# One lookup per pick from a joined expert table, and the second half summed through diagonals on TensorE

## The chip, the core and the metric

The kernel runs on one core of a Trainium2 chip. The metric is the device time of one execution in microseconds, as the median of several runs. The profiles come from single profiled executions of the same program.

## The reference

Two layers of a diffusion backbone for 128 prompt tokens and 256 sample tokens. Each layer is a mixer (attention of two kinds and a short convolution, between projections) and then a feed-forward part in which every token looks up experts by product keys. The change concerns this second part, which the reference computes for chunks of 128 tokens, eight heads and sixteen picks a head:

```python
def one_chunk(xc):
    q = (xc @ wq).reshape(P_CHUNK, P_HEADS, 2, P_HALF)
    sc = jnp.einsum('thcd,hcnd->thcn', q, sub_keys).astype(jnp.float32)
    s1, i1 = lax.top_k(sc[:, :, 0], P_TOPK)
    s2, i2 = lax.top_k(sc[:, :, 1], P_TOPK)
    ...
    top_s, pos = lax.top_k(cand, P_TOPK)
    eidx = jnp.take_along_axis(cand_idx, pos, axis=-1)
    gate = jax.nn.softmax(top_s, axis=-1).astype(xc.dtype)
    u = jnp.take(u_tab, eidx, axis=0)
    act = jax.nn.gelu(jnp.einsum('thkd,td->thk', u, xc))
    vv = jnp.take(v_tab, eidx, axis=0)
    return jnp.einsum('thk,thkd->td', gate * act, vv)
```

All is float32. A token has 8 x 16 = 128 picks, each a row of 1024 values (4 KB) of `u_tab` and one of `v_tab`. Over two layers and three token tiles of 128 tokens that is 2 x 3 x 128 = 768 picks of 128 tokens each, 805 MB out of tables of 16384 rows a layer.

## The kernel before

Tokens lie on the 128 partitions, in three tiles (`T = 3`): tile 0 is the prompt, tiles 1 and 2 the samples. A layer's dense work (norms, projections, attention, output projection, queries and their scores against the keys) is written per group of tiles as a generator `dense_stages(l, tiles)` on each engine, cut into steps; the four stages are P0, S0, P1 and S1 (layer and group). P0's first part runs alone. The rest runs beside the lookups: `Beside` gives each step a weight and calls the next steps whenever their due share of the items is reached. Every engine walks the same list, so that order is fixed by hand and is the same on all of them.

A tile's picks are cut into two units of 64 (`UNIT`), twelve in all. `segments()` lists which unit's first half ("u") and which unit's second half ("v") run together, and beside which dense pieces. `route(n)` on VectorE finds the sixteen picks of a head with searches (L1602 to L1636). The first half: GpSimd issues an indirect DMA that brings row `picks[token]` of `peer_u` to each token's partition, 128 rows of 4 KB (L815), and VectorE multiplies it with the token's activations and sums (`dot`, L1663, with a read of the accumulator). After 64 dots `coefficients(unit)` makes GELU times gate (L1670 to L1679), with ScalarE's tanh (L1278) in the middle. The second half goes another way: TensorE transposes the coefficients (`turn`, L1078) and the picks' numbers (`turn_rows`, L1066), so that the 64 picks of two tokens lie on the 128 partitions; each lookup of `peer_v` (L815 too) brings all picks of a pair of tokens; ScalarE spreads the coefficients over mostly zero columns (`spread`, L1315); and TensorE sums four such lookups at a time with 128x32 matmuls on the four column groups of the array (`add_rows`, L1095) into `ps_acc`. At the end of a tile `feed` (L1687 to L1691) takes the sum, scaled by the modulation gate (a broadcast matmul, L838), into `x`.

Both kinds of lookup share a ring of 14 slots of 4 KB a partition (`RING`); its memory also serves as three extra homes for dense weights before the lookups begin. `lookups()` writes out the order in which GpSimd issues them, and `free_slot` makes it wait for the slot's last reader: VectorE for a "u", TensorE for a "v". The weights come in chunks of 2 MB on SyncE's queue. In float32 a matmul shows as two MATMUL instructions in the profile.

Of the kernel before, what the change touches and what calls it, by code (L numbers as in the profile page):

```python
# [46 lines left out]
HOME_ROWS = KC * NB // DM  # L47
UNIT_HEADS = P_HEADS // 2
UNIT = UNIT_HEADS * TOPK
UNITS_ALL = DEPTH * T * 2  # L50
RING = 14
LEAD = 14
LAG = 12
QUADS = 4
QROWS = P // QUADS
PER = P // UNIT
PARTS = 4
PART = UNIT // PARTS
SPREAD = PART * QROWS + QROWS
GATE_AT = UNIT - 12  # L60
EARLY_ROWS = (1, 5, 7, 11)
ROWS_AT = UNIT - 8
ROWS_HEAD = 2
ROWS_PQ = 9
AHEAD = 2
ROWS = 12
# [29 lines left out]


def after_out(tiles):

    return steps(tiles).index("out") + OUT_CHUNKS * len(tiles)  # L100


SPARSE = 2 * QUADS
EARLY, LATE = (0, UNIT // 2), (UNIT // 2, UNIT)
# [57 lines left out]

class Beside:


    def __init__(self, pieces, programs, items):
        self.steps = [(programs[piece.stage], weight) for piece in pieces for weight in piece.weights]
        self.share = sum(weight for _, weight in self.steps) / items
        self.due, self.done, self.at = 0.0, 0, 0

    def step(self):
        program, weight = self.steps[self.at]
        next(program)
        self.done += weight
        self.at += 1

    def item(self):
        self.due += self.share
        while self.at < len(self.steps) and self.done < self.due - 1e-6:
            self.step()  # L180

    def end(self):
        while self.at < len(self.steps):
            self.step()


class Segment:

    def __init__(self, u, v, beside=None, last=False, rows=(0, UNIT)):
        self.u, self.v, self.beside, self.last = u, v, beside, last
        self.first_row, self.end_row = rows
        self.items = UNIT if u is not None else self.end_row - self.first_row
        self.begins = v is not None and self.first_row == 0
        self.ends = v is not None and self.end_row == UNIT
        self.lag = LAG if u is not None and self.begins else 0
        self.next_u = None

    def rows_added(self, i):  # L200

        if self.v is None:
            return None
        if self.u is not None and self.first_row:
            return self.first_row + i // SPARSE * QUADS if i % SPARSE == SPARSE - 1 else None
        return self.first_row + i - self.lag - QUADS + 1 if i % QUADS == QUADS - 1 and i >= self.lag else None


P0, S0, P1, S1 = (0, P_TILES), (0, S_TILES), (1, P_TILES), (1, S_TILES)


def pieces(name):

    if name is None:
        return (), 1
    if name == "start":
        return (Piece(P0, 0, split_at(P_TILES)),), 1
    if name == "s0_first":
        return (Piece(P0, split_at(P_TILES), None, 2.5), Piece(S0, 0, S0_HALF)), UNIT
    if name == "s0_last":  # L220
        return (Piece(S0, S0_HALF, after_out(S_TILES)),), UNIT
    if name == "s0_end":
        return (Piece(S0, after_out(S_TILES), split_at(S_TILES)),), UNIT // 2
    if name == "s0_rest":
        return (Piece(S0, split_at(S_TILES)),), REST_ITEMS
    if name == "p1":
        return (Piece(P1),), 3 * UNIT + 20
    if name == "s1_first":
        return (Piece(S1, 0, S1_HALF),), UNIT
    if name == "s1_last":  # L230
        return (Piece(S1, S1_HALF, after_out(S_TILES)),), UNIT
    if name == "s1_end":
        return (Piece(S1, after_out(S_TILES), split_at(S_TILES)),), UNIT // 2
    return (Piece(S1, split_at(S_TILES)),), REST_ITEMS


def segments():

    order = (Segment(0, None, "s0_first", True), Segment(1, 0, "s0_last", True),
             Segment(None, 1, "s0_end", True, EARLY), Segment(2, 1, "s0_rest", True, LATE),  # L240
            Segment(3, 2, "p1"), Segment(4, 3, "p1"), Segment(5, 4, "p1"), Segment(None, 5, "p1", True),
            Segment(6, None, "s1_first", True), Segment(7, 6, "s1_last", True),
             Segment(None, 7, "s1_end", True, EARLY), Segment(8, 7, "s1_rest", True, LATE),
            Segment(9, 8), Segment(10, 9), Segment(11, 10), Segment(None, 11))
    for g, after in zip(order, order[1:]):
        g.next_u = after.u
    return order


REST_ITEMS = 40  # L250
S0_HALF = 23
S1_HALF = 20
# [63 lines left out]


HOME, LATEST = homes()
ADA_ORDER = {which: n for n, which in enumerate(c for c in CHUNKS if c[0] == "ada")}

# [50 lines left out]
def pair_of(i):  # L371

    return UNIT // QUADS * (i % QUADS) + i // QUADS
# [1445 lines left out]
```

## Time and profile before

| | |
|---|---|
| time, median of 3 runs (lowest to highest) | 2635.54 us (2628.28 to 2641.29) |
| span of the profiled execution | 2775.9 us |
| bytes moved | 963.23 MB, mean 347 GB/s |
| TensorE, VectorE, GpSimd, ScalarE busy | 1502.5, 1580.1, 1580.2, 284.8 us |
| mean granted clock of TensorE | 0.719 |

The profiled execution is known by its span, from the first to the last instruction; no time around it is shown, so the span is taken as its own time. It is 5.3% above the median of the other runs, and sums made from its rows are brought to that median by the ratio. In the profile a row's first number is busy time (overlaps counted once), then the mean length of one instruction; the idle time behind it is that of the engine just before such instructions. "DMA share" is the mean busy share of sixteen DMA engines. The granted clock is a share of 2.4 GHz.

### The profile page before, as it was taken

To read this page: it belongs to the slowest core of one execution; us is meant where nothing else is said; L and a number is where in the kernel's file an instruction comes from. 1 tells how busy PE (TensorE), PEld (TensorE's weight loads), DVE (VectorE), ACT (ScalarE), POOL (GpSimd) and SP (SyncE) were. 2 spreads that over 40 slices of the span, in tenths; PEclk is the share of its full clock that TensorE was granted. 3 is DMA by queue.
4 is the path that set the end of the run, shared out by engine and by line. 5 is a ranking of instruction groups with operands and counts; after the bars stand their busy time and mean duration, and the time that the engine had idled before them with its cause. 6 is when DMAs were issued, how large, how long until landed. Compare 5 with 4: busy or idle time off the path is not lost.

```text
span 2775.9 us, 21719 instructions
## 1 busy us (share of the span) xinstructions
PE 1502.5 (54%) x6476; PEld 657.2 (24%) x6476; DVE 1580.1 (57%) x3734; ACT 284.8 (10%) x736; POOL 1580.2 (57%) x1601
## 2 busy tenths in 40 slices
PE   6776766867626443445456776686642332232345
PEld 2254323424402111112222234333420000000011
DVE  1348958633767656647446578652668656547410
ACT  1211012211001001000000102211000000000000
POOL 0016526665555566664566785665556666666664
PEclk9888866788857765567777895788865656565567
DMA  9959987899899999998999997999979999999998
GB/s 362 387 204 392 370 310 270 306 371 364 309 381 353 395 357 359 357 353 320 349 369 404 338 391 275 327 333 354 363 292 376 363 359 348 356 364 358 362 372 305
DMA packets 299013, 963.23 MB, mean 347 GB/s; under 512 B 28280, under 2 KB 30712, under 8 KB 298128
## 3 DMA queue, kind: packets, MB, share of 16 engines
q0 software_dynamic: 221184, 805.40, 77.0%
q1 hardware_dynamic: 77712, 156.44, 15.5%
q8 instruction: 53, 0.87, 0.1%
q14 instruction: 64, 0.52, 0.1%
HBM read 959.12 MB, written 2.62 MB: 346 GB/s over the span
## 4 chain that ended last, share of the span: by engine, by line
PE 26%; DMA 19%; DVE 16%; issue 16%; POOL 11%; another core or an unknown queue 10%; ACT 1%; SPq 0%; POOLq 0%; DVEq 0%; ACTq 0%
POOL ring L815 11%; DMA ring<-peer_v,v_rows 9%; PE ps_acc L1095 8%; DVE ring L1663 8%; PE ps_mm L899 5%; DMA ring<-peer_u,u_rows 4%; PE ps_mm L1050 3%; DMA ring<-ada_w 2%; DMA weights<-w_in 2%; PE ps_mm L1020 2%; PE ps_mm L954 2%; DMA weights<-ada_w 1%; PE ps_mb L982 1%; PE ps_acc L858 1%
## 5 line engine op out<-in xcount | busy, mean ns | idle before, releaser
L815 POOL DMA_INDIRECT ring<-peer_v,v_rows x768 | 751.5, 978 | 588.2 <-issue 215.8
L815 POOL DMA_INDIRECT ring<-peer_u,u_rows x768 | 806.1, 1050 | 383.2 <-issue 207.3
L1095 PE MATMUL ps_acc<-ring,coef_cols 128*32 128x512 f32 x3072 | 589.0, 907 | 800.5 <-DMA ring<-peer_v,v_rows 785.8
L1663 DVE CUSTOM_DVE_ANT_0 ring<-ring,ps_tr 128x1024 f32<-128x1024 f32 x512 | 616.6, 1220 | 419.3 <-DMA ring<-peer_u,u_rows 347.8
L1095 PEld LDWEIGHTS ps_acc<-ring,coef_cols 128*32 128x32 f32 x3072 | 117.3, 143 | 1181.4 <-issue 1178.6
L1663 DVE CUSTOM_DVE_ANT_0 ring<-ring,h 128x1024 f32<-128x1024 f32 x256 | 304.9, 1221 | 24.0 <-DMA ring<-peer_u,u_rows 14.7
L1050 PE MATMUL ps_mm<-hT,weights 128*128 128x128 f32 (+1 forms) x1024 | 202.0, 353 | 23.9 <-issue 23.2
L899 PE MATMUL ps_mm<-weights,hT 128*128 128x512 f32 x432 | 199.0, 622 | 17.8 <-DMA weights<-w_in 13.4
L1050 PEld LDWEIGHTS ps_mm<-hT,weights 128*128 128x128 f32 x1024 | 170.8, 211 | 74.6 <-issue 61.4
L776 POOL TENSOR_SCALAR u_rows<-picks 128x16 uint32<-128x16 f32 x48 | 15.9, 330 | 204.2 <-DVE picks L1636 203.2
L899 PEld LDWEIGHTS ps_mm<-weights,hT 128*128 128x128 f32 x432 | 85.5, 200 | 130.8 <-issue 108.9
L1687 DVE TENSOR_TENSOR h<-h,ps_acc 128x1024 f32<-128x1024 f32 x6 | 7.3, 1219 | 190.5 <-PE ps_acc L1095 147.9
L1040 PE MATMUL ps_mb<-proj 128*128 128x128 f32 x160 | 30.7, 314 | 106.5 <-ACT proj L1263 103.3
L954 PE MATMUL ps_mm<-h,scores 32*128 32x384 f32 (+1 forms) x144 | 73.5, 750 | 17.2 <-ACT scores L1208 9.1
L1502 DVE TENSOR_REDUCE negmax<-ps_mm 128x1 f32<-128x384 f32 (+1 forms) x108 | 47.8, 464 | 58.8 <-PE ps_mm L954 35.8
L1020 PE MATMUL ps_mm<-weights,hT 128*128 128x512 f32 x160 | 74.3, 618 | 0.0
L1602 DVE MAX8 half_top<-scores 128x8 f32<-128x128 f32 x96 | 23.3, 284 | 86.6 <-ACT scores L1257 45.6
L1315 ACT ACTIVATE coef_cols<-turned 64x16 f32<-64x16 f32 x96 | 21.9, 228 | 443.8 <-PE ps_acc L1095 386.8
L858 PE MATMUL ps_acc<-weights,condT 128*32 128x512 f32 x224 | 40.4, 862 | 49.8 <-DMA weights<-ada_w 49.8
L1208 ACT ACTIVATE scores<-ps_mm,negmax 128x384 f32<-128x384 f32 (+1 forms) x108 | 54.4, 508 | 107.3 <-DVE negmax L1502 93.2
L1263 ACT ACTIVATE proj<-ps_mm 128x128 f32<-128x128 f32 (+1 forms) x64 | 21.1, 331 | 429.6 <-remote 250.1
L1663 DVE DVE_READ_ACCUMULATOR2_ANT dots<- 128x1 f32 x768 | 63.3, 82 | 0.0
(218 smaller groups left out, 1525.9 us busy)
## 6 DMA issues: line engine op xcount, KB each, us to landing
weights<-w_in SPq DMA_DIRECT2D x17, 2048.0 KB
weights<-peer_wq SPq DMA_DIRECT2D x16, 2048.0 KB
weights<-ada_w SPq DMA_DIRECT2D x14, 2048.0 KB
ring<-ada_w SPq DMA_DIRECT2D x10, 2048.0 KB, 18.0
ring<-peer_u,u_rows POOLq DMA_INDIRECT x768
weights<-w_out SPq DMA_DIRECT2D x6, 2048.0 KB
ring<-peer_v,v_rows POOLq DMA_INDIRECT x768
ring<-w_in SPq DMA_DIRECT2D x3, 2048.0 KB, 20.7
```

The lines of the kernel that those rows point to most:

```text
L815: pool.indirect_dma_start(ring[:, place % RING, :], None, src, bass.IndirectOffsetOnAxis(ap=rows, axis=0)).then_inc(row_full[place % RING] ...
L858: last = pe.matmul(ps_acc[QROWS * j:QROWS * (j + 1), n % 2 * NB:(n % 2 + 1) * NB], condT[:, k, at:at + QROWS], w[:, k, :], start=(i == 0), ...
L899: last = pe.matmul(mm(i), hT[:, k, j * P:(j + 1) * P], w[:, k, :], start=(k == 0), stop=(k == KC - 1))
L954: pe.matmul(scores_at(l, tiles, g, nk * P), q, k, start=True, stop=True, tile_position=(lo, 0)).then_inc(score_mm, 1)
L982: last = pe.matmul(ps_mb[:, col:col + HD], w_.probsT[:, head % 2, s * P:(s + 1) * P], v, start=(s == 0), stop=(s == nk - 1))
L1020: pe.matmul(mm(i), hT[:, k, j * P:(j + 1) * P], w[:, k, :], start=(k == 0), stop=(k == KC - 1))
L1040: last = pe.matmul(key_scores_at(l, tiles, i, nt * P)[:, j * P:(j + 1) * P], pqT[:, i % 4, j * P:(j + 1) * P], keysT[:, i, :], start=True, ...
L1050: last = pe.matmul(mm(i, nt * P), w[:, k, (i % 4) * P:(i % 4 + 1) * P], hT[:, k, 0:nt * P], start=(k == 0), stop=(k == KC - 1))
L1095: last = pe.matmul(ps_acc[QROWS * k:QROWS * (k + 1), b * NB:(b + 1) * NB], coef_cols[:, i // PART % 2, at:at + QROWS], ring[:, slot("v", n ...
L1208: act.activation(w_.probs[:, probs_slot(head, second), 0:nk * P], scores_at(l, tiles, g, nk * P), ACT.Exp, bias=negmax[:, u:u + 1], accum_ ...
L1502: dve.tensor_reduce(negmax[:, u:u + 1], scores_at(l, tiles, j * UNITS + u, nk * P), AXX, ALU.max, negate=True).then_inc(negmax_ready, 1)
L1663: dve.tensor_tensor_reduce(row, row, h, 1.0, 0.0, ALU.mult, ALU.add, dots[:, n // UNIT % 2, n % UNIT:n % UNIT + 1]).then_inc(u_used, 1)
```

## The change

The tables `peer_u` and `peer_v` become one table a layer, `peer_uv0` and `peer_uv1`, whose row is 8 KB: the u row and behind it the v row. One lookup a pick brings both to the token's partition, 1 MB a lookup. The ring has 9 slots of 8 KB a partition (`SLOTS`). Rows are no longer turned to other partitions: TensorE adds `diag(coefficient of pick n) @ v rows of pick n` into `ps_acc`, with two 128x128 matmuls of 512 columns a pick, whose diagonal ScalarE makes from the identity and the coefficient as a scale (`diagonals`). Coefficients are made for two picks at a time (`GROUP = 2`): `polynomial(g)` behind the second dot, tanh on ScalarE, `coefficients(g)` behind the dense steps of that item. TensorE adds a pair one pair later (`LATE_GROUPS = 1`). Gates are handled per head, with the sum taken by the exponential. `segments()` and `lookups()` go; one loop over 768 picks remains, with the dense pieces at ranges of picks (`sides()`). Modulation sums of later stages go to `ps_mb`, because `ps_acc` is in use from the first pick on. The area for the lookups' descriptors is given as 4096 bytes.

```diff
-RING = 14
-LEAD = 14
-LAG = 12
+SLOTS = 9
+HOME_SLOTS = KC * NB // (2 * DM)
+TILE = P_HEADS * TOPK
+PICKS = DEPTH * T * TILE
...
+GROUP = 2
+LATE_GROUPS = 1
+FEED_AT = 2
+DIAGS = 6
 AHEAD = 2
...
+def sides():
+
+    return ((0, 104, (Piece(P0, split_at(P_TILES), None, 2.5), Piece(S0, 0, split_at(S_TILES)))),
+            (TILE, TILE + 40, (Piece(S0, split_at(S_TILES)),)),
+            (TILE + 40, 3 * TILE - 32, (Piece(P1),)),
+            (3 * TILE + 4, 3 * TILE + 104, (Piece(S1, 0, split_at(S_TILES)),)),
+            (4 * TILE, 4 * TILE + 40, (Piece(S1, split_at(S_TILES)),)))
...
@@ gpsimd
-            for place, (table, n) in enumerate(LOOKUPS):
-                if table == "u":
-                    if n % TOPK == 0:
-                        take_head(n // TOPK)
...
+            for n in range(PICKS):
+                if n % TOPK == 0:
+                    pool.wait_ge(picks_ready, n // TOPK + 1)
                     pool.sem_inc(gather_may, 1)
...
+                if n >= SLOTS:
+                    pool.wait_ge(v_used, n - SLOTS + 1)
+                    pool.sem_inc(gather_may, 1)
+                picks = rows[:, n // TOPK % HEADS_KEPT, n % TOPK:n % TOPK + 1]
+                pool.indirect_dma_start(ring[:, n % SLOTS, :], None, peer_uv1 if n >= PICKS // 2 else peer_uv0,
+                                        bass.IndirectOffsetOnAxis(ap=picks, axis=0)).then_inc(row_full[n % SLOTS], 16)
@@ tensor
-                for b in range(2):
-                    for k in range(QUADS):
-                        at = (k * PART // QUADS + r % (PART // QUADS) + 1) * QROWS - PER - PER * r
-                        last = pe.matmul(ps_acc[QROWS * k:QROWS * (k + 1), b * NB:(b + 1) * NB],
-                                         coef_cols[:, i // PART % 2, at:at + QROWS], ring[:, slot("v", n + k), b * NB:(b + 1) * NB],
-                                         start=(r == 0), stop=(r == UNIT // QUADS - 1), tile_position=(0, QROWS * k))
-                last.then_inc(v_used, QUADS)
+                pe.wait_ge(diag_ready, n + 1)
                 for b in range(2):
+                    last = pe.matmul(ps_acc[:, b * NB:(b + 1) * NB], diags[:, n % DIAGS, :],
+                                     ring[:, n % SLOTS, DM + b * NB:DM + (b + 1) * NB], start=(i == 0), stop=(i == TILE - 1))
+                last.then_inc(v_used, 1)
...
+            for i in range(PICKS):
+                side.item(i)
+                if i % GROUP == GROUP - 1 and i // GROUP >= LATE_GROUPS:
+                    add_group(i // GROUP - LATE_GROUPS)
+                if i >= TILE and i % TILE == FEED_AT - 1:
+                    gate_sum_rows(i // TILE - 1)
@@ scalar
+            def diagonals(g):
+                act.wait_ge(coef_ready, g + 1)
+                for n in range(g * GROUP, (g + 1) * GROUP):
+                    if n >= DIAGS:
+                        act.wait_ge(v_used, n - DIAGS + 1)
+                    act.activation(diags[:, n % DIAGS, :], ident, ACT.Copy, scale=of_head(coef, n)).then_inc(diag_ready, 1)
@@ vector
+            def polynomial(g):
+
+                n = g * GROUP
+                a, some = of_head(dots, n, GROUP), of_head(poly, n, GROUP)
+                dve.wait_ge(u_used, n + GROUP)
+                step.after(dve.scalar_tensor_tensor(out=some, in0=a, scalar=GELU_A, in1=a, op0=ALU.mult, op1=ALU.mult))
+                dve.scalar_tensor_tensor(out=some, in0=some, scalar=1.0, in1=a, op0=ALU.add, op1=ALU.mult).then_inc(poly_ready, 1)
...
+                step.after(dve.scalar_tensor_tensor(out=of_head(gated, n, GROUP), in0=a, scalar=gate_inv[:, head % 2:head % 2 + 1],
+                                                    in1=gates_of(head)[:, k:k + GROUP], op0=ALU.mult, op1=ALU.mult))
+
+            def coefficients(g):
+
+                n = g * GROUP
+                dve.wait_ge(tanh_ready, g + 1)
+                dve.scalar_tensor_tensor(out=of_head(coef, n, GROUP), in0=of_head(poly, n, GROUP), scalar=1.0,
+                                         in1=of_head(gated, n, GROUP), op0=ALU.add, op1=ALU.mult).then_inc(coef_ready, 1)
...
+                dot(i)
+                if i % GROUP == GROUP - 1:
+                    polynomial(i // GROUP)
+                side.item(i)
+                if i % GROUP == GROUP - 1:
+                    coefficients(i // GROUP)
+                if i >= TILE and i % TILE == FEED_AT:
+                    feed(i // TILE - 1)
@@ kernel()
-    arrays["peer_u"] = a["peer_u"].reshape(DEPTH * N_EXPERTS, DM)
-    arrays["peer_v"] = a["peer_v"].reshape(DEPTH * N_EXPERTS, DM)
+    for l in range(DEPTH):
+        arrays[f"peer_uv{l}"] = np.concatenate([a["peer_u"][l], a["peer_v"][l]], axis=1)
```

## Rows read from the trace of the kernel before

**Rows 1.** Busy time of the engines, from the page.

```profile
PE 1502.5 (54%) x6476; PEld 657.2 (24%) x6476; DVE 1580.1 (57%) x3734; ACT 284.8 (10%) x736; POOL 1580.2 (57%) x1601
```

**Rows 2.** DMA queues: packets, MB, share of sixteen engines' span.

```profile
q0 software_dynamic: 221184, 805.40, 77.0%
q1 hardware_dynamic: 77712, 156.44, 15.5%
```

**Rows 3.** By stretch: us, PE, PEld, DVE, ACT, POOL busy; clock, DMA share, GB/s.

```profile
0.00:200.00 200.00, 144.74 (x679) 70.07 (x680) 59.62 (x163) 34.18 (x93) 3.40 (x7) 0.86 0.86 314
200.00:672.00 472.00, 345.91 (x1388) 174.50 (x1387) 312.47 (x729) 81.49 (x193) 266.47 (x242) 0.78 0.92 339
...
1549.00:1950.00 401.00, 296.66 (x1108) 145.80 (x1108) 251.45 (x494) 77.91 (x179) 264.99 (x232) 0.81 0.91 335
...
2130.00:2776.00 646.00, 219.65 (x1038) 44.57 (x1038) 310.35 (x715) 13.03 (x46) 415.31 (x446) 0.62 0.95 355
```

**Rows 4.** A window of 20 us with lookups alone.

```profile
2120.00:2140.00 20.00, 0.80 (x3) 0.20 (x2) 18.41 (x41) 1.63 (x7) 14.48 (x17) 0.58 1.02 410
```

**Rows 5.** DMA queues of four stretches: 0:200, 200:672, 1549:1950, 2130:2776.

```profile
q1 hardware_dynamic: 32222, 62.71, 86.2%
...
q0 software_dynamic: 32968, 120.07, 68.6%
q1 hardware_dynamic: 19426, 39.52, 22.9%
...
q0 software_dynamic: 31976, 116.41, 78.6%
q1 hardware_dynamic: 8665, 17.62, 11.9%
...
q0 software_dynamic: 62716, 228.34, 94.2%
```

**Rows 6.** Windows of L1095 alone: PE and PEld busy.

```profile
200.00:672.00 472.00, 64.11 (x384) 12.99 (x384) 0.78 0.92 339
1549.00:1950.00 401.00, 60.64 (x368) 12.33 (x368) 0.81 0.91 335
```

**Rows 7.** Pieces of the chain: start us, us, what.

```profile
1830.13 7.06 PE ps_mm L1020 x16
...
2116.88 3.49 PE ps_acc L838 x4
```

**Rows 8.** Waits of PE, 200:672: us in total, times, longest.

```profile
PE ps_acc L858 <- DMA weights<-ada_w: 29.4, 6, 12.7
...
PE ps_tr L877 <- DVE merged L1410: 8.0, 2, 6.2
```

**Rows 9.** Waits of PE, 1549:1950.

```profile
PE ps_mm L899 <- DMA weights<-w_in: 9.3, 2, 4.7
PE ps_tr L877 <- DVE h L1410: 8.3, 2, 6.9
```

**Rows 10.** Groups of instructions: busy us, mean ns, idle before.

```profile
L1663 DVE CUSTOM_DVE_ANT_0 ring<-ring,ps_tr 128x1024 f32<-128x1024 f32 x512 | 616.6, 1220 | 419.3 <-DMA ring<-peer_u,u_rows 347.8 <-issue 33.1 <-remote 18.8
L1663 DVE DVE_READ_ACCUMULATOR2_ANT dots<- 128x1 f32 x768 | 63.3, 82 | 0.0
L1509 DVE RECIPROCAL rinv<-rowsum 128x2 f32<-128x2 f32 x36 | 5.8, 160 | 2.0 <-ACT scores L1208 1.6 <-issue 0.3
L1297 ACT ACTIVATE turned<-ps_acc 128x128 f32<-128x128 f32 x12 | 3.3, 278 | 2.3 <-PE ps_acc L1078 1.6 <-issue 0.5
```

**Rows 11.** Timeline of VectorE: end of one head's routing and of the next.

```profile
1448.99 0.19 DVE L1636 SCALAR_TENSOR_TENSOR picks<-pair_key 128x32 f32<-128x32 f32 x1
...
1458.17 0.19 DVE L1636 SCALAR_TENSOR_TENSOR picks<-pair_key 128x32 f32<-128x32 f32 x1
```

**Rows 12.** Timeline: one unit's coefficients, first and last operation.

```profile
2278.92 0.23 DVE L1670 TENSOR_TENSOR poly<-dots 128x64 f32<-128x64 f32 x1
...
2280.04 0.29 DVE L1679 SCALAR_TENSOR_TENSOR coef<-poly,dots 128x128 f32<-128x128 f32 x1 [0.25 <-issue]
```

More of the change, by code:

```diff
@@ L160, in __init__ @@
         self.weights = [weight or weights[kind] for kind in kinds[first:last]]
-class Beside:
[L166 to L184, printed above, removed]
@@ L187 @@
[L187 to L206, printed above, removed]
@@ L209 @@
[L209 to L234, printed above, removed]
@@ L237, in segments @@
[L237 to L247, printed above, removed]
@@ new lines, with __init__, item @@
+class Beside:
+    def __init__(self, programs):
+        self.programs, self.at = programs, [0] * len(sides())
+        self.done = [0.0] * len(sides())
+    def item(self, i):
+        for s, (first, end, pieces) in enumerate(sides()):
+            if not first <= i < end:
+                continue
+            order = [(piece.stage, weight) for piece in pieces for weight in piece.weights]
+            due = sum(weight for _, weight in order) * (i + 1 - first) / (end - first)
+            while self.at[s] < len(order) and (self.done[s] < due - 1e-6 or i == end - 1):
+                stage, weight = order[self.at[s]]
+                next(self.programs[stage])
+                self.done[s] += weight
+                self.at[s] += 1
@@ L255, in ada, with start @@
+def start(programs):
+    for _ in range(split_at(P_TILES)):
+        next(programs[P0])
 def ada(l, first, last):
@@ L842, in modulate @@
             def modulate(which):
-                assert not made["turned"]
                 made[which[0]] += 1
@@ L971, in weigh_values @@
                             pe.wait_ge(conv_read, nth(l, tiles, 1, j))
-                        if head == A_HEADS and j == nt - 1 and early_row(l, tiles) is not None:
-                            pe.wait_ge(rows_ready, early_row(l, tiles) + 1)
                         for s in range(nk):
@@ L996, in dense_stages @@
                             weigh_values(head - 2)
-                        if early_row(l, tiles) is not None and j == nt - 1 and head == ROWS_HEAD:
-                            turn_rows(early_row(l, tiles))
                         yield "head"
@@ L1224, in dense_stages @@
                             exps(head + 1)
-                        if early_row(l, tiles) is not None and j == nt - 1 and head == ROWS_HEAD:
-                            copy_rows(early_row(l, tiles))
                         yield "head"
@@ L1265, in dense_stages @@
                         copy_scores(i - 1)
-                    if (l, tiles) == P1 and i == ROWS_PQ:
-                        copy_rows(2 * T - 1)
                     if i == 15:
@@ new lines, in _ @@
+            start(programs)
+            side = Beside(programs)
+            for n in range(AHEAD):
+                for _ in route(n):
+                    pass
+                if n == 0:
+                    gate_top(0)
+            routing = iter(())
+            for i in range(PICKS):
+                head, k = i // TOPK, i % TOPK
+                if k == TOPK // 2:
+                    for _ in routing:
+                        pass
+                    routing = route(head + AHEAD) if head + AHEAD < ALL_HEADS else iter(())
+                next(routing, None)
+                if k == 2 and head + 1 < ALL_HEADS:
+                    gate_top(head + 1)
+                dot(i)
+                if i % GROUP == GROUP - 1:
+                    polynomial(i // GROUP)
+                side.item(i)
+                if i % GROUP == GROUP - 1:
+                    coefficients(i // GROUP)
+                if i >= TILE and i % TILE == FEED_AT:
+                    feed(i // TILE - 1)
```

435 lines of the change are left out of this document (98 added, 337 removed).

## The prediction

> **What bounds the kernel now.** The order of reading was the page's busy line, its DMA queues, and then windows by stretch; groups, waits and pieces of the chain came after them, for durations. TensorE, VectorE and GpSimd are each busy for 54 to 57% of the span [rows 1], but the lookups' queue fills 77.0% of the sixteen DMA engines' time and the weights' queue 15.5% [rows 2]: together 92.5% of 2775.9 us. The windows [rows 3] tell the stretches apart. Lookups start at about 200 us. In the stretch that is nearly lookups alone, 2130 to 2776, the DMA share is 0.95 at 355 GB/s with PE at 34% and DVE at 48%: transfers set the pace. In the two stretches that hold the sample tiles' dense work (200 to 672 and 1549 to 1950) the share drops to 0.92 and 0.91 while PE is busy for 73 and 74% of the time: there the dense work already costs transfers something. I call a "pick" one expert of 128 tokens with both its rows, 1.0486 MB; there are 768, before as two lookups and after as one.
>
> **Transfers.** Bytes don't change; packets do. Two queues give two equations: 221184 packets and 805.40 MB took 77.0% of 16 x 2775.9 us, and 77712 packets and 156.44 MB took 15.5% [rows 2]. They solve to 6.9 ns a packet and 40.6 us a MB of one engine's time. After, there are half as many lookup packets, so 110592 x 6.9 ns / 16 = 48 us of transfer time go. A pick falls from 2137/768 = 2.78 us to 2.72 us at a full DMA. Bounds: nothing gained (2.78), and the fastest window that shows only lookups, 410 GB/s at share 1.02 [rows 4], which is 2.56 us a pick before that saving and 2.50 after it. I take 2.72, because it stands on all packets. How full is the DMA? Now 0.95 in the lookup stretch. The ring goes from 14 half-size slots (7 MB) to 9 full ones (9 MB), and GpSimd, busy for 415 of 646 us there [rows 3], issues half as many lookups; I take 0.98, so 2.72/0.98 = 2.775 us a pick. The same stretch runs now at 646 us for 228.34 MB [rows 3, 5], 2.97 us a pick. GpSimd's own saving, half of its busy time, is worth nothing by itself: the transfers cover it.
>
> **TensorE.** Removed: the 128x32 matmuls (64.1 and 60.6 us busy in the two dense stretches [rows 6]) and the transposes of coefficients and rows. Added: each pick is two full 128x128 matmuls of 512 columns, and the chain shows how such a float32 matmul is two instructions: 16 took 7.06 us, 4 took 3.49 us [rows 7]. So a pick costs 4 instructions: 1.77 us at the 2.4 GHz level, 3.49 us where the engine had been mostly idle and the clock was at its lower level (1.2 GHz). 768 picks are 1359 us at the fast level, in place of 589. In the lookup stretches 1.77 is under 2.775 and hides; if the clock drops, PE falls behind, becomes busy, and the dense stretches show what a busy PE is granted (0.78 and 0.81 as means [rows 3]). In the dense stretches it doesn't hide. There PE has its own work in front of each pair of picks:
> - first sample stretch: 345.9 - 64.1 = 281.8 us of other PE work, which the new schedule spreads over picks 0 to 104; plus 104 x 1.77 = 184; plus waits that stay, 29.4 for modulation weights and 8.0 on VectorE [rows 8]: 503 us. Transfers alone would want 104 x 2.72 + 39.52 MB x 2.75 us = 392 us (2.75 us a MB is 430 us for 156.44 MB [rows 2]), so PE is the bound.
> - second: 296.7 - 60.6 = 236.0 us of other work, 100 picks x 1.77 = 177, waits 9.3 + 8.3 [rows 9]: 431 us, against 320 for transfers.
> Before, these stretches took 472 and 401 us and carried 120.07 and 116.41 MB [rows 3, 5], that is 114.5 and 111 picks. After, they carry fewer picks in more time. That is the loss which I set against the gain elsewhere.
>
> **VectorE and ScalarE.** Per pair of picks VectorE does two dots, 2 x (1.220 + 0.082) [rows 10]; one eighth of a head's routing, 9.18 us from one head's last operation to the next [rows 11]; and a chain of four small operations with a tanh of ScalarE in the middle, which now comes 384 times and not 12. Now it takes 1.41 us on 64 columns, from 2278.92 to 2280.33 [rows 12]. Two columns cost about what the reciprocal on two columns does, 160 ns [rows 10]; the bounds are 4 x 0.16 = 0.64 and 1.41; I take 1.0 us. With some 0.25 us of gaps a pair is 5.0 us, so 2.5 us a pick: under 2.775, but with only 10% to spare. If an operation or the wait for tanh costs more, what is late is the coefficient, then the diagonal, then the slot, which is not free before TensorE has read it. Behind the waiting coefficient stand the next dots and routing. ScalarE adds 768 diagonals at some 278 ns [rows 10] and 384 tanh: about 310 us on an engine that is 10% busy, at no cost to the end. The gate's maximum and exponential per head, the per-head reciprocal and one 1.2 us addition less per tile are within 20 us and hidden. The modulation sums that go to another PSUM tile wait for nothing new. The smaller descriptor area only matters if nine lookups in flight do not fit, for which nothing speaks.
>
> **The sum**, in the profiled execution's time: 200 up to the first lookup, as before; 503; 431; the other 768 - 204 = 564 picks x 2.775 = 1565; the weights outside the three named stretches, 156.44 - 62.71 - 39.52 - 17.62 = 36.6 MB [rows 2, 5] x 2.75 = 101; and 20 us for the end (the last pair's chain, its matmuls, gate and store). That is 2820 us against 2776, 1.6% more. The median of the runs, 2635.5, is 0.949 of the profiled span, so about **2677 us**.
>
> A rule that speaks against any gain stands in the Trainium skill, HBM Reference, "Specifications (TRN2)": some 358 GB/s effective per core. By it a pick could never take less than 2.93 us, whatever its packets; the 355 GB/s of the lookup stretch looks like it [rows 3], the 410 GB/s window disagrees [rows 4]. The case is rival 1, worked out there from rows alone.
>
> **Rivals.**
> 1. No gain per pick: lookups keep their present 2.97 us, because what limits them is not packets or issue. For it: PE, DVE and POOL all have room in that stretch and it still runs at 355 GB/s. Against: the 20 us window at 410 GB/s. Then 564 x 0.19 = 107 more: 2927, so 2779 us.
> 2. The faster side: picks outside the dense stretches run at the burst pace, 2.50/0.98 = 2.55 us. Place: those 564 picks; price -0.225 x 564 = -127 us; 2693, so 2557 us. It decides from 2.70 us a pick: there the sum equals 2776. For it: that window [rows 4], and the deeper ring. Against: VectorE's 2.5 us leaves nothing over. The Trainium skill (DMA: Bandwidth & Descriptors, "Where 436 GB/s comes from") gives a ceiling of 435 GB/s, by which a pick would take 2.41 us; no row reaches it.
> 3. A full-rate clock in the dense stretches. PE's other work there was measured at 0.78 and 0.81. Fully busy, it could shrink to at best 220 and 191 us, 107 us off: 2713, so 2576 us. For it: 0 to 200 us had 0.86 at 72% busy [rows 3]. Against: part of that work is small instructions and latencies that don't scale.
> 4. VectorE as the bound: pairs at 6.0 us, 3.0 a pick, 127 us more: 2947, so 2798 us. This takes 0.5 us a pick more than my count.
> 5. A slow clock throughout: the lookup stretch had 0.62 [rows 3]. If TensorE got no more than the 1.2 GHz level there, a pick would take 3.49 us: 564 x 0.715 = 403 more, 3223, so 3060 us. Against: busier stretches had 0.78 and more, and here PE would be busy all the time. The Trainium skill (TensorE: Matmul & The Clock Gate, Part 1) says that the low rate is the default and activity releases it; the trace agrees, with 0.62 where PE is busy 34% and 0.86 at 72% [rows 3].
>
> **How the numbers follow.** This kernel's runs spread over 0.5%, so less can't be told from no change: 2622 to 2649 us is "same". Chances: my forecast (2650 to 2750) 0.38; rival 2 or 3, alone or in part, 0.34; halves of them that end within 0.5%, 0.13; rival 1 0.07, rival 4 0.06, rival 5 0.02. So faster 0.34, same 0.13, slower 0.53. The range reaches down past rivals 2 and 3 (2557, 2576), leaving out that both hold fully, and up past 1 and 4: 2540 to 2800. The forecast's own range is 2650 to 2750.
>
> **What would show it.** Lookup packets at 110592 and the queue's share times span near 2090 us; in the last stretch a pick per 2.7 to 2.8 us with DMA share 0.97 or more. The stretch from the first lookup to pick 104 near 500 us, PE busy over 90% of it, GpSimd idle for TensorE; DMA share there under 0.85. PE busy in total over 2000 us. VectorE at 2.5 us a pick in lookup stretches. The prediction is wrong if PE's other work shrinks with a faster clock, if packets cost more than 6.9 ns each, or if VectorE's small chain costs over 1.5 us a pair.

## The result, and the profile after

The changed kernel takes 2686.8 us (median of 4 runs, 2686.34 to 2690.32) beside 2634.3 us for the kernel before on the same chip: a ratio of 1.0204, 95% interval 1.0184 to 1.0223. It is 2% slower on that chip; the experiments show that this side doesn't hold on every chip. On two later occasions it took 2690.4 and 2686.9 us, with ratios of 1.0217 and 1.0209. The forecast was 2677 us.

From the page of the changed kernel: its span, the busy line, and the lookups' and weights' queues (packets, MB, share of sixteen engines). They answer to [rows 1, 2].

```profile
span 2684.8 us, 23465 instructions
...
PE 2230.6 (83%) x6452; PEld 1073.4 (40%) x6452; DVE 1793.1 (67%) x5249; ACT 600.2 (22%) x1836; POOL 789.9 (29%) x773
...
q0 software_dynamic: 110592, 805.36, 74.7%
q1 hardware_dynamic: 77712, 156.44, 15.9%
```

Half the lookup packets and the same bytes, as the change says; TensorE's busy time grows by 728 us and GpSimd's halves, against [rows 1].

The same page, groups of the new work (busy us, mean ns, idle before and what ended it):

```profile
L904 PE MATMUL ps_acc<-ring,diags 128*128 128x512 f32 x3072 | 1456.2, 624 | 218.2 <-ACT diags L1084 215.2
L656 POOL DMA_INDIRECT ring<-peer_uv,rows x768 | 787.9, 1026 | 1864.6 <-PE ps_acc L904 1515.5
...
L1077 ACT ACTIVATE poly<-poly 128x2 f32<-128x2 f32 x384 | 77.6, 202 | 1163.3 <-DVE poly L1414 1163.1
L1084 ACT ACTIVATE diags<-consts,coef 128x128 f32<-128x128 f32 x768 | 265.5, 393 | 115.9 <-DVE coef L1425 113.7
L1425 DVE SCALAR_TENSOR_TENSOR coef<-poly,gated 128x2 f32<-128x2 f32 x384 | 61.9, 161 | 221.5 <-ACT poly L1077 220.0
```

GpSimd has become a waiter: 1515.5 us of its idle time end when TensorE has read a slot. That alone doesn't say that TensorE is the bound, since with a full ring this wait is there too when transfers set the pace. The windows decide. Windows of the changed kernel (us; PE, PEld, DVE, ACT, POOL busy; clock, DMA share, GB/s): the start, the stretch from the first lookup to pick 104, the second sample stretch (picks 388 to 488), and the lookups alone at the end. They answer to [rows 3].

```profile
0.00:200.00 200.00, 139.89 (x640) 65.52 (x641) 56.82 (x152) 34.56 (x92) 2.30 (x6) 0.89 0.86 312
200.00:695.00 495.00, 427.91 (x1407) 219.71 (x1407) 301.58 (x840) 123.18 (x346) 126.90 (x108) 0.92 0.82 305
...
1539.00:1955.00 416.00, 375.08 (x1123) 190.10 (x1122) 281.84 (x788) 115.74 (x320) 113.96 (x98) 0.95 0.77 289
...
2128.00:2670.00 542.00, 417.44 (x871) 166.30 (x869) 418.26 (x1259) 101.27 (x347) 202.56 (x211) 0.96 1.00 412
```

And the lookups' queue in the last three of these stretches (packets, MB, share), which answers to [rows 5]:

```profile
q0 software_dynamic: 15280, 111.29, 59.4%
...
q0 software_dynamic: 14021, 102.11, 65.0%
...
q0 software_dynamic: 30627, 222.99, 99.5%
```

The kernel before was profiled again on a chip on which it takes as long as in the timed runs above (2632 us). Its span there is 2627.2 us. The same stretches and queue rows of that execution:

```profile
200.00:665.00 465.00, 341.26 (x1398) 171.72 (x1397) 313.65 (x735) 83.25 (x199) 268.94 (x243) 0.79 0.93 345
1485.00:1885.00 400.00, 307.17 (x1151) 152.83 (x1152) 257.74 (x521) 79.09 (x183) 261.33 (x233) 0.80 0.92 339
...
2044.00:2600.00 556.00, 204.15 (x978) 40.95 (x974) 294.70 (x677) 13.02 (x46) 399.54 (x432) 0.61 1.01 392
```

```profile
q0 software_dynamic: 33080, 120.50, 69.3%
...
q0 software_dynamic: 32159, 117.10, 79.2%
...
q0 software_dynamic: 59748, 217.57, 100.4%
```

**Where the time went.** The two sample stretches went from 465 and 400 us with 120.50 and 117.10 MB of lookups to 495 and 416 us with 111.29 and 102.11 MB. At 1.0486 MB a pick that is 46 us more for 23 picks fewer, and those picks cost 2.6 us each later on: 106 us lost. Elsewhere the kernel before took 2627 - 200 - 865 = 1562 us for 541 picks, the changed one 2685 - 200 - 911 = 1574 us for 564. With some 98 us for weights in both, a pick falls from 2.70 to 2.62 us, which gives 48 us back. The difference is the 58 us between the two spans. The ends of the stretches are read by hand (in two executions of one kernel, further below, the first came to 454 and 448 us), so the split is good to some 6 us. At the end, with lookups alone, a pick falls from 556/207.5 = 2.68 to 542/212.7 = 2.55 us.

### The profile page after: what moved, and what is told of

Its sections match the earlier page's. It is cut to its first block, busy times and chain, and to the rows that moved or that the text cites. A ratio compares the mean times of both kernels' runs of the same rounds, so it can differ in the third digit from the quotient of the medians.

```text
span 2684.8 us, 23465 instructions
## 1 busy us (share of the span) xinstructions
PE 2230.6 (83%) x6452; PEld 1073.4 (40%) x6452; DVE 1793.1 (67%) x5249; ACT 600.2 (22%) x1836; POOL 789.9 (29%) x773
## 3 DMA queue, kind: packets, MB, share of 16 engines
q0 software_dynamic: 110592, 805.36, 74.7%
HBM read 959.12 MB, written 2.62 MB: 358 GB/s over the span
## 4 chain that ended last, share of the span: by engine, by line
PE 47%; DMA 22%; DVE 21%; issue 5%; ACT 3%; POOL 1%; SPq 0%; DVEq 0%; POOLq 0%; ACTq 0%
PE ps_acc L904 24%; DMA ring<-peer_uv,rows 17%; DVE ring L1406 8%; PE ps_mm L739 7%; PE ps_mm L886 5%; PE ps_mm L858 3%; DMA ring<-ada_w 2%; PE ps_mm L796 2%; POOL ring L656 1%; DMA weights<-w_in 1%; DMA weights<-peer_wq 1%; DMA weights<-ada_w 1%; PE ps_mb L679 1%; DVE poly L1413 1%; ACT poly L1077 1%
## 5 line engine op out<-in xcount | busy, mean ns | idle before, releaser
L904 PE MATMUL ps_acc<-ring,diags 128*128 128x512 f32 x3072 | 1456.2, 624 | 218.2 <-ACT diags L1084 215.2
L656 POOL DMA_INDIRECT ring<-peer_uv,rows x768 | 787.9, 1026 | 1864.6 <-PE ps_acc L904 1515.5
L904 PEld LDWEIGHTS ps_acc<-ring,diags 128*128 128x128 f32 x3072 | 591.5, 199 | 997.7 <-issue 645.9
L1077 ACT ACTIVATE poly<-poly 128x2 f32<-128x2 f32 x384 | 77.6, 202 | 1163.3 <-DVE poly L1414 1163.1
L1084 ACT ACTIVATE diags<-consts,coef 128x128 f32<-128x128 f32 x768 | 265.5, 393 | 115.9 <-DVE coef L1425 113.7
L1425 DVE SCALAR_TENSOR_TENSOR coef<-poly,gated 128x2 f32<-128x2 f32 x384 | 61.9, 161 | 221.5 <-ACT poly L1077 220.0
L886 PE MATMUL ps_mm<-hT,weights 128*128 128x128 f32 (+1 forms) x1024 | 188.4, 341 | 17.6 <-DMA weights<-peer_wq 9.3
L1418 DVE SCALAR_TENSOR_TENSOR gated<-dots,gate_inv,pair_top 128x2 f32<-128x2 f32 x384 | 83.0, 216 | 1.7
L1414 DVE SCALAR_TENSOR_TENSOR poly<-poly,dots 128x2 f32<-128x2 f32 x384 | 62.2, 162 | 13.4
L1413 DVE SCALAR_TENSOR_TENSOR poly<-dots 128x2 f32<-128x2 f32 x384 | 61.7, 161 | 13.3
L796 PE MATMUL ps_mm<-h,scores 32*128 32x384 f32 (+1 forms) x144 | 49.3, 543 | 11.1 <-ACT scores L1009 7.5
## 6 DMA issues: line engine op xcount, KB each, us to landing
ring<-ada_w SPq DMA_DIRECT2D x10, 2048.0 KB, 16.6
```

The costliest lines, as they stand in the source:

```text
L656: pool.indirect_dma_start(ring[:, n % SLOTS, :], None, peer_uv1 if n >= PICKS // 2 else peer_uv0, bass.IndirectOffsetOnAxis(ap=picks, axis ...
L796: pe.matmul(scores_at(l, tiles, g, nk * P), q, k, start=True, stop=True, tile_position=(lo, 0)).then_inc(score_mm, 1)
L886: last = pe.matmul(mm(i, nt * P), w[:, k, (i % 4) * P:(i % 4 + 1) * P], hT[:, k, 0:nt * P], start=(k == 0), stop=(k == KC - 1))
L904: last = pe.matmul(ps_acc[:, b * NB:(b + 1) * NB], diags[:, n % DIAGS, :], ring[:, n % SLOTS, DM + b * NB:DM + (b + 1) * NB], start=(i == ...
L1077: act.activation(some, some, ACT.Tanh, scale=GELU_B).then_inc(tanh_ready, 1)
L1084: act.activation(diags[:, n % DIAGS, :], ident, ACT.Copy, scale=of_head(coef, n)).then_inc(diag_ready, 1)
```

## The experiments

**Is the kernel before the same everywhere?** Two runs of it, unaltered.

> The kernel before, unchanged, profiled once more. Theory: its first profiled execution (span 2775.9 us) was slower than its runs, because the one of the changed kernel has a span of 2684.8 us at a time of 2686.6 us. Then this one has a span of about its time, near 2635 us, and the 140 us are missing above all in lookup stretches, which then run above 355 GB/s. Rival: the profiler itself costs this kernel 5% (it has twice the lookups), then the span is near 2776 us again.

Measured: 2772.7 us (2756.58 to 2792.44) on one chip, span 2772.1.

> The kernel before, unchanged, for a profile that stands on the same chip as the others of this job. Its span should equal its time within 2 us, as in the last job (2772.1 at 2772.7). If it runs near 2634 us here, theory 1 wants its 4 KB packets shorter than the 172.8 ns mean of the slow chip's profiles, and its dense stretches hardly changed; rival 2 wants them longer or shorter everywhere.

Measured on another chip: 2631.9 us (2619.57 to 2642.61), span 2627.2. So the kernel before takes 2773 us on one chip and 2632 on another, and in both cases the profiled execution is as long as the timed ones. The first of the two expectations failed in both its theories: not only the profiled execution was long there, every timed run was. By their lengths, the span of 2775.9 us that the prediction was built on belongs to the first kind of chip and the median of 2635.5 to the second; which chips these were isn't known. Windows with lookups alone, on the first chip (columns as above), with their queue row:

```profile
2130.00:2700.00 570.00, 188.88 (x866) 37.68 (x870) 301.76 (x696) 12.57 (x44) 375.79 (x405) 0.59 0.96 361
...
q0 software_dynamic: 56514, 205.78, 96.2%
```

That is 570/196.2 = 2.90 us a pick, against 2.68 on the other chip. Only about half of this difference is longer packets: the queue's share times the time is 2.79 us a pick here and 2.69 there. The rest is time in which the DMA engines moved nothing (share 0.96 against 1.01).

**Does the joined lookup give the pace?** The changed kernel, but with the tables apart and two lookups of 4 KB rows a pick into the same slot:

```diff
-                pool.indirect_dma_start(ring[:, n % SLOTS, :], None, peer_uv1 if n >= PICKS // 2 else peer_uv0, ...)
+                for half in range(2):
+                    pool.indirect_dma_start(ring[:, n % SLOTS, half * DM:(half + 1) * DM], None, tables[half], ...)
...
-            return (n // SLOTS + 1) * 16
+            return (n // SLOTS + 1) * 32
```

> The changed kernel, but each pick takes two lookups of 4 KB rows from two tables into the two halves of its slot. Theory 1 (packets): a pick gets dearer by the 6.9 ns of 128 more packets, 0.06 us, which is 34 us over the 564 picks outside the dense stretches: about 2720 us, with lookup stretches at some 407 GB/s in place of 417. Rival 2 (depth of the ring alone): nothing changes, 2687 us within 10. Rival 3 (GpSimd): a lookup costs it 1.24 us from issue to issue, 2.48 us a pick, nearly the pace of 2.56 us, and with its waits it becomes the bound: 2.7 us a pick or more, over 2760 us.

Measured: 2848.0 us, beside 2772.8 for the kernel before on the same chip (the first kind), ratio 1.0294 (1.0234 to 1.0355). Windows of this kernel: the two sample stretches and the end.

```profile
200.00:699.00 499.00, 433.89 (x1395) 218.94 (x1395) 301.29 (x835) 122.68 (x345) 232.90 (x214) 0.90 0.84 302
1603.00:2020.00 417.00, 376.03 (x1125) 190.53 (x1124) 282.60 (x790) 116.46 (x320) 222.88 (x198) 0.95 0.81 291
2217.00:2830.00 613.00, 435.74 (x867) 175.44 (x865) 415.88 (x1258) 101.40 (x347) 399.93 (x422) 0.90 0.96 363
```

The sample stretches are nearly as long as in the changed kernel (499 and 417 against 495 and 416 us on the other kind of chip): there the form of the lookup hardly matters. The end falls back to 363 GB/s, the kernel before's pace on this chip (361), though the ring is 9 MB. So without the joined row the rest of the change costs 2.9% here, and the joined row gives the pace back. Its price is far above theory 1's 34 us, if the changed kernel takes some 2690 us on this chip too, and the time lies where rival 3 put it, over 2760 us. This run doubles two things at once, the packets and GpSimd's issues, and doesn't separate them. GpSimd was busy for 399.93 of 613 us at the end, and only 36 us of its idle time there were waits for a slot. On the faster chip the kernel before issued as many lookups a pick at 2.68 us a pick, so GpSimd's work alone doesn't explain the 2.89 us of this run; how the gain is shared between fewer packets and fewer issues stays open.

**What does TensorE's sum cost beside the dense work?** The second matmul of a pick (columns 512 to 1023 of the sum) is left out, for picks 0 to 103 and 384 to 487 in one kernel, and for all other picks in a second.

```diff
-                for b in range(2):
+                beside = 104 if tau in (0, 3) else 0
+                for b in range(1 if i < beside else 2):
```

> The changed kernel without the second of the two matmuls of a pick for picks 0 to 103 and 384 to 487, so columns 512 to 1023 of these picks are left out of the sum. Theory (TensorE is the bound of the two dense stretches): each of these 204 picks saves 0.88 us, 92 and 92 us at most; the first stretch falls from 495 to about 405 us, the second from 416 to about 330, and the time to about 2515 us. Rival (the waits between engines in the dense steps set these stretches, or the transfers do): under 40 us in all, 2650 us or more.

> The changed kernel without the second matmul of a pick everywhere but in the two dense stretches (picks 0 to 103 and 384 to 487) and at each tile's first and last pick; half of the columns of those picks are left out of the sum. Theory: TensorE is hidden behind transfers there, the time stays within 15 us of 2687 us. Rival (TensorE, 70 to 80% busy there, also bounds those stretches, with its wait for the late pair): the time falls by more than 60 us.

Measured: 2621.4 us for the first, 65 us less than the changed kernel, and 2670.3 us for the second, 17 us less though it leaves out nearly three times as many matmuls. Both ran on the first kind of chip and the changed kernel on the second; on a chip of the second kind the first of them took 2616.3 us (below), 71 us less than the changed kernel there. TensorE is the bound in the sample stretches and nearly hidden elsewhere. But the gain is far from the 2515 us expected: halving 373 us of sum in those stretches took 152 us off the sum's busy time and freed only 71. Windows of the first of the two kernels, and under them TensorE's work on `ps_acc` alone in the same windows:

```profile
200.00:654.00 454.00, 356.90 (x1188) 184.60 (x1187) 299.36 (x826) 122.53 (x345) 116.55 (x107) 0.87 0.86 329
1504.00:1890.00 386.00, 313.25 (x927) 160.71 (x926) 281.31 (x788) 115.67 (x320) 108.98 (x99) 0.88 0.82 315
```

```profile
200.00:654.00 454.00, 111.50 (x205) 0.87 0.86 329
1504.00:1890.00 386.00, 110.30 (x201) 0.88 0.82 315
```

The same two rows of the changed kernel:

```profile
200.00:695.00 495.00, 190.75 (x400) 0.92 0.82 305
1539.00:1955.00 416.00, 182.57 (x393) 0.95 0.77 289
```

In the first stretch TensorE's sum fell by 79 us and the stretch by 41. Its other work rose from 427.91 - 190.75 = 237 to 245 us at a lower granted clock (0.92 to 0.87), and its idle time from 67 to 97 us: more of the waits for weights and for other engines is uncovered, the one for modulation weights for example 22.1 us in place of 16.6.

**A cheaper form of the sum.** ScalarE scales the v row itself (128x1024, in place of the 128x128 diagonal) into a float32r tile, and TensorE adds it with the identity: one instruction for 512 columns in place of two. A slot is free as soon as ScalarE has read it, and no longer when TensorE has. Memory then holds 8 slots and not 9.

```diff
-SLOTS = 9
+SLOTS = 8
+SCALED = 2
...
-                    last = pe.matmul(ps_acc[:, b * NB:(b + 1) * NB], diags[:, n % DIAGS, :], ring[:, n % SLOTS, DM + ...], ...)
+                    last = pe.matmul(ps_acc[:, b * NB:(b + 1) * NB], ident_r[:], scaled[:, n % SCALED, b * NB:(b + 1) * NB], ...)
...
-                    act.activation(diags[:, n % DIAGS, :], ident, ACT.Copy, scale=of_head(coef, n)).then_inc(diag_ready, 1)
+                    act.activation(scaled[:, n % SCALED, :], ring[:, n % SLOTS, DM:], ACT.Copy, scale=of_head(coef, n)).then_inc(row_scaled, 1)
```

> The changed kernel with another way to the sum: ScalarE scales the v rows of a pick by its coefficient (128x1024, rounded to float32r) and TensorE adds them with the identity as two float32r matmuls, one instruction each. 8 slots in place of 9, two scaled buffers in place of six diagonals, and a slot is free as soon as ScalarE has read it. Theory (TensorE's 1.77 us a pick is what the dense stretches lack): TensorE falls to some 0.5 us a pick, 1300 us less in all; the first dense stretch goes from 495 to its other PE work and waits, about 380 to 420 us, the second from 416 to about 320 to 340, the rest stays, so about 2530 us. Rival (e2 took 92 us off each stretch and gave back only 48 and 30, so waits between engines and a slower clock take over): about 2600 us. Second rival: ScalarE's 1.0 us a pick in its fixed order delays the attention steps, over 2650 us.

Measured: 2618.7 us beside 2633.2 for the kernel before, ratio 0.9934 (0.9911 to 0.9958). It beats both, the kernel before by a little (0.7%). The time is near the first rival's 2600 us and not the theory's 2530; the sum took 743.6 us of TensorE in all, in place of 1456.2, which is 0.97 us a pick and 713 us less, where 0.5 us and 1300 us had been expected. Beside it the changed kernel ran again:

> The changed kernel, unchanged, beside the kernel before on one chip. The kernel before has now been seen at 2634 us and, in another job, at 2773 us. Theory 1 (chips differ in what lookups of 4 KB rows cost, and 8 KB rows don't feel it): the changed kernel takes 2687 us within 10 again, whatever the kernel before takes here, so the ratio is 1.02 where that is near 2634 and 0.97 where it is near 2773. Rival 2 (the slower chip is slower for both): 2687 x 1.05 = 2825 us where the kernel before takes 2773.

Measured: 2690.4 us, ratio 1.0217 (1.0178 to 1.0256). So this form is worth 72 us, the cheaper sum, the earlier release of the slot and the slot less taken together; no run separates them. Windows of the kernel with scaled rows, whole and for `ps_acc` on TensorE alone:

```profile
200.00:661.00 461.00, 350.57 (x1214) 206.76 (x1213) 301.22 (x837) 200.08 (x346) 114.81 (x110) 0.79 0.86 326
1498.00:1889.00 391.00, 313.05 (x931) 185.83 (x929) 281.57 (x787) 191.47 (x321) 107.10 (x99) 0.77 0.80 302
2061.00:2608.00 547.00, 244.75 (x432) 108.02 (x432) 418.25 (x1262) 262.62 (x349) 203.26 (x211) 0.50 0.99 411
```

```profile
200.00:661.00 461.00, 81.49 (x205) 0.79 0.86 326
```

TensorE's sum fell by 109 us in the first stretch, the stretch by 34. TensorE's other work rose from 237 to 269 us (clock 0.92 to 0.79) and its idle time from 67 to 110. At the end it ran at 1.2 GHz throughout (0.50) and that cost nothing, because a pick's sum still fits under the transfer.

**The depth of the ring.**

> The changed kernel with a ring of 7 slots of 8 KB in place of 9, so 7 MB as the kernel before has. Theory (the depth of 9 MB is not what brings the pace): lookup stretches stay at 2.5 to 2.6 us a pick, the time rises by under 30 us. Rival (depth carries the gain): lookup stretches fall to 2.8 us a pick or more, over 100 us more.

> The ring has 8 slots in place of 9, all else as in the changed kernel. Seven slots cost 60 us. If each slot less costs the same, this is 2715 to 2722 us (ratio to the changed kernel 1.011); if the cost comes only below some depth, 2685 to 2700 us. Rival: nine lookups in flight are too many for the transfers and eight are as good or better, 2670 to 2690 us.

Measured: 2750.2 us with seven slots and 2701.2 with eight, against 2690.4 and 2686.9 with nine beside them. The cost is not even: 14 us for the first slot, then some 46 to 49 (seven and eight slots ran on two chips of the second kind). The 60 us for seven slots are twice what the expectation allowed, and far under its rival's 100. The windows of seven slots show that the end hardly suffers:

```profile
1572.00:1995.00 423.00, 380.80 (x1135) 193.01 (x1134) 282.45 (x785) 116.20 (x320) 116.00 (x101) 0.95 0.77 288
2178.00:2730.00 552.00, 411.87 (x866) 163.49 (x865) 418.22 (x1256) 101.28 (x347) 204.55 (x212) 0.97 0.99 407
```

The end takes 10 us more and each sample stretch 3 to 7. The larger part of the 61 us of span lies in the stretches between: the one behind the first sample stretch took 874 us at a DMA share of 0.95, where it took 844 at 0.98 with nine slots. That dense work holds up TensorE for a while there and the ring has to bridge it would explain this, but isn't shown. Seven slots are also as much memory as the ring of the kernel before has. At the end they run at 407 GB/s against its 392 on the same kind of chip, so of the 412 GB/s with nine slots the depth of the ring gives the last 5.

**Do the chips differ for every kernel, or for the lookups of 4 KB rows?** The changed kernel, the scaled rows and the kernel without half of the sum beside the dense work were run once more.

> The changed kernel unaltered, for a comparison with the kernel before on whichever chip this is. Theory A (the chips differ in what a 4 KB packet costs and not in what an 8 KB packet costs): the changed kernel takes 2680 to 2695 us on any chip; where the kernel before takes about 2635 here the ratio is 1.02 again, where it takes about 2770 here the ratio is 0.97. Theory B (such a chip is slower for every kernel by the same factor): the ratio is 1.02 in both cases, so 2825 us beside 2770.

> The kernel with rows scaled on ScalarE and added by TensorE in the cheaper float32r form, a second time, with its 8 slots. Theory A: 2610 to 2630 us on any chip, so a ratio of 0.99 to the kernel before where that takes 2635 and 0.945 where it takes 2770. Against the same kernel with diagonals and 8 slots beside it in this job, the sum's form alone is worth 80 to 100 us; against 9 slots 68 us. Theory B (chip slower by one factor for every kernel): 2750 us where the kernel before takes 2770.

> The kernel that leaves out the sum of columns 512 to 1023 for the picks beside the sample tiles' dense work (0 to 103 and 384 to 487), run a second time. The first time it took 2621.4 us beside 2773 us for the kernel before. Theory A (where the kernel before takes 2773 rather than 2635, only its 4 KB packets are slower): this kernel takes 2615 to 2630 us also beside a kernel before of 2635. Theory B (one factor for every kernel): it takes 2621 x 2635 / 2773 = 2491 us there.

All three fell on a chip on which the kernel before takes 2634 or 2628 us, so the first two only repeat: 2686.9 us (ratio 1.0209) and 2620.1 us (ratio 0.9946, 0.9921 to 0.9971; 81 us under the diagonals with the same eight slots). The third kernel tells the theories apart. On the first kind of chip it had taken 2621.4 us beside 2773; here it took 2616.3 us beside 2628.2. One factor for every kernel would have made it 2485 us. It moved by 0.2% while the kernel before moved by 5.5%. The windows of its end are alike too, on the first chip and on this one:

```profile
2062.00:2604.00 542.00, 419.31 (x871) 167.25 (x869) 417.61 (x1256) 101.29 (x347) 202.91 (x211) 0.95 1.00 412
```

```profile
2056.00:2599.00 543.00, 415.62 (x871) 165.57 (x869) 417.78 (x1256) 101.28 (x347) 203.13 (x211) 0.96 1.00 411
```

So this kernel with 8 KB rows is as fast on both kinds of chip, and the kernel before, with 4 KB rows, is not. The changed kernel itself was never run on the first kind. If it too moves by 0.2% only, it would be some 3% faster than the kernel before there (an estimate: about 2690 against 2773 us). The first kind was met on one chip and in one series of runs, besides the first profile; whether the chip is the cause, or something else of that series such as where the tables lay in memory, isn't shown. "Kind of chip" stands here for what the kernel before took beside a run.

## Why the prediction was right, and where it was not

The time and the side came out, 2677 against 2687 us. The mechanism of the sample stretches was right; the pace of the transfers and the conversion were wrong, and their errors offset each other. The time within 10 us is luck, and so in part is the side. Within the profiled frame the prediction said 2820 against 2776 us, 1.6% slower; its terms measured 2685 us, which is 3% less than 2776. The kernel came out slower because the runs it was compared with came from the faster kind of chip.

- **The sample stretches** were forecast at 503 and 431 us and took 495 and 416. The mechanism holds: TensorE is their bound and the sum doesn't hide there (65 us from half of it, against 17 us elsewhere). The terms inside were off. TensorE's other work was 237 us and not 281.8 in the first, and 375.08 - 182.57 = 192.5 and not 236.0 in the second: rival 3's faster clock came nearly whole, 0.92 and 0.95 against 0.78 and 0.81 [rows 3], and the work shrank by as much as the clock rose. The sum took 191 and 183 us against 184 and 177. The waits took 67 and 41 us against 37.4 and 17.6. TensorE's waits in the first stretch (us in total, times, longest), which answer to [rows 8]:

```profile
PE ps_mb L698 <- DMA weights<-ada_w: 16.6, 5, 7.0
PE ps_mm L886 <- DMA weights<-peer_wq: 9.3, 1, 9.3
PE ps_tr L717 <- DVE h L1164: 8.3, 2, 6.9
PE ps_tr L845 <- DVE merged L1322: 8.0, 2, 6.2
PE ps_tr L876 <- ACT proj L1062: 6.1, 1, 6.1
```

  The wait for modulation weights shrank, and waits for projections' weights and for other engines came in its place. "PE busy over 90%" was wrong in the first (86%) and just met in the second (90%).
- **Transfers** are the step that failed. The term was 2.775 us a pick outside the sample stretches, 1565 us, with 101 for weights and 20 for the end: 1686 us. It took 1574. At the end the pace was that of rival 2 (2.55 us), 412 GB/s at a share of 1.00, and 2.62 us on average outside the sample stretches. The price of 6.9 ns a packet was too low. The lookups' queue took 0.797 x 2627.2 = 2094 us before on the faster chip and 0.747 x 2684.8 = 2006 after, where 2090 was forecast; 88 us x 16 over 110592 packets is 12.7 ns for each packet saved. Against the first profile (0.770 x 2775.9 = 2137 us) it is 19 ns. The queue before, on the faster chip:

```profile
q0 software_dynamic: 221184, 805.40, 79.7%
```

  The two equations had solved for packets and bytes from two queues with different kinds of transfer, and gave a number that neither had.
- **The conversion** by 0.949 was wrong in kind. It was read as the difference between a profiled and a timed execution; by the repeated runs it was the difference between two kinds of chip, which the kernel with 4 KB rows feels and one with 8 KB rows doesn't. Applied to terms that don't depend on the chip it took off 143 us, and the errors in the terms were 8 + 15 + 112 = 135 us the other way. The hit within 10 us is owed to that and to nothing else.
- **VectorE** was forecast at 2.5 us a pick; at the end it is busy for 418.26 us in 212.7 picks, 1.97 us. The small chain was right (four operations of 160 to 216 ns are 0.70 us a pair, with tanh in between; 1.0 was taken). Without dots (1.30 us) and the chain (0.35) 0.31 us a pick is left, 5 us a head, where 9.18 had been read from one head's end to the next [rows 11]: that interval must have held other work than routing. So rival 4 was further off than it seemed. These lines of VectorE's timeline (start, us) show a pair's chain; VectorE waits 0.21 us for tanh:

```profile
2300.08 0.16 DVE L1413 SCALAR_TENSOR_TENSOR poly<-dots 128x2 f32<-128x2 f32 x1
2300.27 0.16 DVE L1414 SCALAR_TENSOR_TENSOR poly<-poly,dots 128x2 f32<-128x2 f32 x1
2300.35 0.22 DVE L1418 SCALAR_TENSOR_TENSOR gated<-dots,gate_inv,pair_top 128x2 f32<-128x2 f32 x1
2300.78 0.16 DVE L1425 SCALAR_TENSOR_TENSOR coef<-poly,gated 128x2 f32<-128x2 f32 x1 [0.21 <-ACT poly L1077]
```

- **What wasn't foreseen** is that tanh stands behind dense work in ScalarE's fixed order. In the first stretch VectorE waits 59.5 us for it in 29 waits, the longest 10.4 us:

```profile
DVE coef L1425 <- ACT poly L1077: 59.5, 29, 10.4
```

  In the longest of these, up to 315.92 us, ScalarE itself was waiting, 11.48 us for a projection on TensorE, and TensorE was busy all that time. In the whole stretch TensorE waited for a diagonal once, for 0.4 us. So the late coefficients themselves cost next to nothing there. Whether VectorE's waits made its dense results late, for which TensorE waits in the list above, isn't shown. Where the sum was halved, VectorE waited less for tanh (37.5 us), but TensorE 4.2 us for diagonals.
- **Rival 1** (nothing gained per pick) is refuted, and with it the figure of 358 GB/s per core as a bound: the end ran at 412 GB/s. The Trainium skill, HBM Reference, "Specifications (TRN2)", says under the figure that a core that streams alone measures about 425 GB/s; the 412 GB/s of the end come near that and lie well above the table's figure, and the prediction had used the table alone. **Rival 5** fell too: the clock rose to 0.96 at the end.

**What stays open.** Why one chip, or one series of runs, takes 4 KB rows more slowly. How much of the joined row's gain comes from fewer packets and how much from GpSimd's fewer issues. And what the joined row is worth by itself on the faster chip: the kernel with two lookups was run on the first kind only (2848 us). If its ratio of 1.0294 held on the other, it would take 2712 us there, and the joined row would be worth 25 us; the pace per pick outside the sample stretches, 2.70 to 2.62 us, speaks for 48.

## What to carry to other kernels

Before work is moved to an engine that is "half idle", find the stretches in which it isn't: there each microsecond added is paid, here 106 us for 204 picks, while the transfers' gain is earned only in the others. Gather in rows as long as the data allows: 8 KB rows ran at 412 GB/s (407 with a ring as small as before) where 4 KB rows ran at 392 or 361, depending on the chip. Then make the sum in the cheapest form that the moved-to engine has, and give the rest to an engine with room: rows scaled on ScalarE turned 2% slower into 0.5 to 0.7% faster, with the slot free earlier as part of it.

## What the runs showed of the hardware

- Runs on two chips differ by 5% for a kernel that gathers rows of 4 KB (2773 and 2632 us) and by 0.2% for one that gathers rows of 8 KB (2621.4 and 2616.3 us). A ratio between two such kernels is valid only for the chip on which both ran.
- Part of what is gained by taking work from TensorE is lost again to its clock. With 79 and 109 us less of the sum in the first sample stretch the granted clock fell from 0.92 to 0.87 and 0.79, and the same other work took 245 and 269 us in place of 237. Only 41 and 34 us of the stretch were gained; waits took the rest.
- A float32 matmul of 512 columns is two instructions, 624 ns long on average in the changed kernel; they overlap, so the 3072 of the sum kept TensorE busy for 1456.2 us, 1.90 us a pick. In float32r it is one instruction: 1536 in all and 743.6 us, 0.97 us a pick, much of it at a lower clock.
